# Banded attention: the division by the sums moved from VectorE to GpSimd, and the output copies moved ahead of the transposed tiles' copies

## What is computed

```python
s = einsum('bnqkgd,bnjkd->bnkgqj', qb, kb) * (Dh ** -0.5)
s = s - slopes * dist;  s = where(in_window & real_key, s, -inf)
m = maximum(s.max(axis=-1), sink)
p = exp(s - m[..., None])
denom = p.sum(axis=-1) + exp(sink - m)
p = p / denom[..., None]
o = einsum('bnkgqj,bnjkd->bnqkgd', p, vb)
```

## Time and profile before

| what | value |
|---|---|
| time, median of 3 runs | 3200.48 us (3200.15 to 3201.1) |
| time of the profiled execution | 3194.09 us |
| its span (first to last instruction) | 3192.2 us |
| TensorE busy | 3029.1 us |
| VectorE busy | 1512.5 us |
| ScalarE busy | 738.1 us |
| GpSimd busy | 15.9 us in 30 instructions |

### The profile page before, as it was taken

One profiled execution on the slowest core, in us unless ns is written; L12 is line 12 of the kernel. 1 busy time (PEld: TensorE's weight loads), 2 busy tenths in 40 slices (PEclk: granted clock), 3 DMA queues, 4 the chain that ended last, 5 costly groups with the idle time before them and its releaser, 6 DMA issues.

```text
span 3192.2 us, 37105 instructions
## 1 busy us (share of the span) xinstructions
PE 3029.1 (95%) x15055; PEld 2235.0 (70%) x15055; DVE 1512.5 (47%) x2327; ACT 738.1 (23%) x1397; POOL 15.9 (0%) x30
## 2 busy tenths in 40 slices
PE   6999999999899999979999998999999997899999
PEld 4888888868755888854443433468888845788887
DVE  2577766726566345451101122356554427645544
ACT  4343434321076110120000012332000025300001
POOL 0000000000000000000000000000000000000000
PEclk8999999999999999989999999999999998999999
DMA  5145334342200122249999981102222220122221
GB/s 224 71 182 196 139 139 177 120 161 74 96 14 8 78 108 80 79 163 391 421 422 422 422 342 69 53 27 79 80 79 106 80 81 27 53 79 80 81 104 53
DMA packets 64234, 451.80 MB, mean 142 GB/s; under 512 B 7248, under 2 KB 7264, under 8 KB 11216
## 3 DMA queue, kind: packets, MB, share of 16 engines
q1 hardware_dynamic: 61200, 439.38, 34.5%
q0 software_dynamic: 2080, 7.11, 0.7%
q10 hardware_dynamic: 800, 3.15, 0.3%
HBM read 445.41 MB, written 2.10 MB: 140 GB/s over the span
## 4 chain that ended last, share of the span: by engine, by line
PE 85%; DMA 6%; DVE 5%; ACT 2%; issue 1%; DVEq 1%; SPq 0%; PEldq 0%; PEld 0%; POOL 0%; ACTq 0%; POOLq 0%
PE PS L228 77%; DMA ring<-stream 4%; PE PS L1508 1%; PE PS L1618 1%; PE PS L1601 1%; DVE arena L1570 1%; DMA hT<-stream 1%; DVE stat L1627 1%; PE PS L2273 1%; PE PS L2293 1%; DVE stat L2620 0%; PE PS L2276 0%; DVE PS L2618 0%; ACT arena L1537 0%; PE PS L873 0%
## 5 line engine op out<-in xcount | busy, mean ns | idle before, releaser
L228 PE MATMUL PS<-arena 128*128 128x256 f32 (+3 forms) x4960 | 986.2, 389 | 9.0 <-issue 4.9
L228 PEld LDWEIGHTS PS<-arena 128*128 128x128 f32 (+1 forms) x4960 | 744.3, 183 | 237.8 <-issue 156.6
L228 PE MATMUL PS<-arena,ring 128*128 128x256 f32 (+1 forms) x1992 | 466.7, 390 | 0.3 <-issue 0.3
L228 PE MATMUL PS<-hT,ring 128*128 128x256 f32 (+1 forms) x1504 | 409.8, 428 | 23.7 <-ACT hT L323 11.5
L228 PEld LDWEIGHTS PS<-arena,ring 128*128 128x128 f32 x1992 | 377.6, 190 | 74.6 <-issue 26.5
L228 PEld LDWEIGHTS PS<-hT,ring 128*128 128x128 f32 x1504 | 289.8, 194 | 130.2 <-issue 86.7
L228 PE MATMUL PS<-xT,arena 128*128 128x256 f32 x1056 | 232.0, 379 | 0.0
L228 PEld LDWEIGHTS PS<-xT,arena 128*128 128x128 f32 x1056 | 200.6, 190 | 28.1 <-issue 1.0
L228 PE MATMUL PS<-ring,arena 128*32 128x512 f32 (+3 forms) x1088 | 198.2, 590 | 12.1 <-issue 6.5
L228 PE MATMUL PS<-hT,arena 128*128 128x256 f32 (+1 forms) x864 | 195.2, 442 | 1.3 <-DMA hT<-stream 1.3
L2092 DVE TENSOR_TENSOR arena<-arena,PS 128x512 f32<-128x512 f32 x16 | 11.0, 688 | 368.3 <-PE PS L228 368.3
(11 more groups left out here) (307 smaller groups left out, 2946.9 us busy)
## 6 DMA issues: line engine op xcount, KB each, us to landing
ring<-stream SPq DMA_DIRECT2D x283, 1024.0 KB, 6.9
arena<-stream SPq DMA_DIRECT2D x96, 1024.0 KB, 18.8
hT<-stream SPq DMA_DIRECT2D x32, 1024.0 KB, 18.7
arena<-stream SPq DMA_DIRECT2D x8, 512.0 KB, 5.0
arena<-x ACTq DMA_DIRECT2D x1, 2048.0 KB, 10.6
xT<-stream SPq DMA_DIRECT2D x2, 1024.0 KB, 15.4
arena<-arena POOLq DMA_DIRECT2D x16, 128.0 KB, 2.6
arena<-x POOLq DMA_DIRECT2D x1, 2048.0 KB, 12.5
```

The costliest lines, as they stand in the source:

```text
L228: ins = nc.tensor.matmul(out_, lhsT, rhs, start=start, stop=stop_, **kw)
```

## The change

In the attention with a sink, DVE stops after the reciprocal (which now overwrites the sums) and signals the new semaphore `a_r`; GpSimd waits for it, does the four multiplications in place, and signals `a_n`, for which the transposes wait as before. ScalarE's output copies of a finished head group are issued ahead of the copies of the current unit's transposes. The sink's value gets four places in turn (in the rows `RECIP` and `SINK`) in place of two. The two semaphores of `iota` and `router` become one, `in_route`, and both waits are for both loads.

```diff
+        def sink_of(u):
+            return stat[:, RECIP + u % 4 // 2, u % 2, :]
...
+            a_r = sem(f"{name}_r") if sink else None
...
-                        nc.scalar.activation(col(SINK, u), col(SINK, u), ACT.Exp)
+                        nc.scalar.activation(sink_of(u), sink_of(u), ACT.Exp)
...
                     if u + 1 < n:
                         exps(u + 1)
+                    for i, m in enumerate(last_unit):
+                        if m == u - 2 and sink:
+                            outputs(i)
                     copies(u)
                     for i, m in enumerate(last_unit):
-                        if m == u - 2:
+                        if m == u - 2 and not sink:
                             outputs(i)
...
                 def normalise(u):
                     v.wait_ge(a_e, u + 1)
                     if sink:
-                        nc.vector.tensor_tensor(col(SUM, u), col(SUM, u), col(SINK, u), ALU.add)
+                        nc.vector.tensor_tensor(col(SUM, u), col(SUM, u), sink_of(u), ALU.add)
                         v.drain()
+                    if sink:
+                        nc.vector.reciprocal(col(SUM, u), col(SUM, u)).then_inc(a_r, 1)
+                        return
...
+            def pool_(pool):
+                for u in range(n):
+                    pool.wait_ge(a_r, u + 1)
+                    for h in range(nh):
+                        x = norm_io(u, h)
+                        ins = nc.gpsimd.tensor_scalar(x, x, col(SUM, u)[:, h:h + 1], None, ALU.mult)
+                    ins.then_inc(a_n, 1)
...
-            pe.wait_ge(in_router, 16)
+            pe.wait_ge(in_route, 32)
...
-            v.wait_ge(in_iota, 16)
+            v.wait_ge(in_route, 32)
...
             pool.dma_start(snk[:, 0, :], sinks).then_inc(in_swa, 16)
+            swa_att_pool(pool)
```

More of the change, by code:

```diff
@@ L199, in build @@
         evac_done = sem("evac_done")
-        in_const, in_vec, in_x, in_c, in_cst2, in_acst, in_iota = (sem(n) for n in
-            ("in_const", "in_vec", "in_x", "in_c", "in_cst2", "in_acst", "in_iota"))
+        in_const, in_vec, in_x, in_c, in_cst2, in_acst, in_route = (sem(n) for n in
+            ("in_const", "in_vec", "in_x", "in_c", "in_cst2", "in_acst", "in_route"))
         vec_t, vec_ok, cs_ok, ada_sel = (sem(n) for n in ("vec_t", "vec_ok", "cs_ok", "ada_sel"))
@@ L1558, in peak @@
                     v.wait_ge(a_s, u + 1)
-                    maximum(v, u, S2[u % 2], col(MAX, u), col(NEGMAX, u), col(SINK, u)).then_inc(a_m, 1)
+                    maximum(v, u, S2[u % 2], col(MAX, u), col(NEGMAX, u), sink_of(u)).then_inc(a_m, 1)
                 def normalise(u):
@@ L1578, in dve_ @@
                         peak(u + 2)
-            return pe_, act_, dve_, a_o, a_s
+            def pool_(pool):
[5 more added lines that the diff above has]
+                    ins.then_inc(a_n, 1)
+            return pe_, act_, dve_, a_o, pool_ if sink else a_s
         def tile_of(a, i):
@@ L1852, in build @@
         idxu = sb("idxu", [NE, CAP], u32)
-        in_router, r_lg, r_sum, r_mx, r_ex, r_aff, r_affT, r_tt, r_blk, r_row, r_ok = (sem(n) for n in
-            ("in_router", "r_lg", "r_sum", "r_mx", "r_ex", "r_aff", "r_affT", "r_tt", "r_blk", "r_row", "r_ok"))
+        r_lg, r_sum, r_mx, r_ex, r_aff, r_affT, r_tt, r_blk, r_row, r_ok = (sem(n) for n in
+            ("r_lg", "r_sum", "r_mx", "r_ex", "r_aff", "r_affT", "r_tt", "r_blk", "r_row", "r_ok"))
         e_g, e_xs, e_gu, e_sg, e_hid, e_T, e_hT, e_dn, e_ys, e_cb, e_acc = (sem(n) for n in
@@ L2624, in swa_maximum @@
             return nc.vector.tensor_tensor(extra, neg, snk[:, 0, 4 * g:4 * g + 4], ALU.add)
-        swa_att_pe, swa_att_act, swa_att_dve, swa_out, _ = attention(
+        swa_att_pe, swa_att_act, swa_att_dve, swa_out, swa_att_pool = attention(
             "swa", 16, 4, swa_score, swa_chunk, swa_dest, [[u] for u in range(16)], swa_value,
@@ L2707, in _ @@
             pool.wait_ge(x_ok, 1)
-            pool.dma_start(iota_s, iota).then_inc(in_iota, 16)
-            pool.dma_start(rw, router).then_inc(in_router, 16)
+            pool.dma_start(iota_s, iota).then_inc(in_route, 16)
+            pool.dma_start(rw, router).then_inc(in_route, 16)
             pool.wait_ge(x_ok, 2)
```

## The result

The changed kernel is slower: 3216.1 us in the median of 6 executions (3211.94 to 3217.66) against 3200.32 (3191.82 to 3201.69) for the kernel before, a ratio of 1.0052 [1.0039, 1.0065]. Forecast were 3197.2 us and a range up to 3211; the time lies beyond it. The profiled execution of the changed kernel took 3211.94 us, its span is 3209.7.

What follows compares the result with a forecast made beforehand. VectorE was taken to pace each 17.74 us head group; a ring of 16.87 us saves 0.87 a group, 3.3 us over 15 / 4 groups, all else 0: 3200.5 - 3.3 = 3197.2 us. Range 3190 to 3211.

Steps and rivals of the forecast that it cites:

- 4P + 4P': GpSimd's eight scalings in a head group: P a full one, taken as 0.46 us, P' a short one, 0.37.
- rival 2: Each GpSimd scaling costs like a DMA issue, 0.80 us: 3209.6 us, chance 0.25; its lower-clock extreme 3230 us, 0.03.
- rival 1: GpSimd scales as quickly as VectorE (P = 0.30, P' = 0.22): 3192.6 us, chance 0.3.
- the even ring: Loop of waits through peaks of even units: 11.51 + 2H + 8P, 16.09 us a head group.
- the tail: After the last unit's exponentials, scalings free the transposes after 2.7 us; they started 3.3 us after before: nothing added.
- the ring: Loop of waits from VectorE's reciprocal through GpSimd's scalings and TensorE to VectorE's peak, two turns a head group, at full clock.
- H: Pair of hand-offs, VectorE to GpSimd and GpSimd to TensorE: taken as 0.45 us, bounds 0.10 and 0.60.
- the odd ring: Loop of waits through peaks of odd units, the slower: 12.65 + 2H + 4P + 4P', 16.87 us a head group.
- VectorE's own 16.5: VectorE's own work for a head group in the kernel before: 16.5 us of 17.74.
- The output copies: ScalarE's output copies, issued earlier: the values' wait for them disappears, with TensorE's 1.87 us and the slow clock behind it.
- rival 4: VectorE's small SBUF instructions at a peak's end and GpSimd's scalings exclude each other, meeting over P = 0.56; no own chance.
- rival 3: GpSimd's first scaling stalls once for a code fetch, 7.2 us: 3204.4 us, chance 0.05.

Runs made afterwards that it cites:

- e5: The changed kernel with 12 idle transposes of the identity (the fill) on TensorE ahead of each unit's wait for the scalings: 3204.26 us, ratio 1.0017 to the kernel before.
- e4: The changed kernel with VectorE waiting for the last scaling before its sums for the next stage: 3209.48 us, ratio 1.004 to the kernel before.
- e9: The changed kernel with GpSimd scaling only 128 columns of each head, plus 8 idle transposes ahead of each unit's wait: 3204.44 us, ratio 1.0012 to the kernel before.
- e14: The changed kernel with 8 idle transposes a unit, a first signal after two scalings, and VectorE's last sums behind the last scaling: 3201.32 us, ratio 1.0003.
- e10: The kernel before with output copies moved first and 6 idle transposes ahead of each unit's wait, no scalings on GpSimd: 3190.82 us, ratio 0.9978.
- e1: The kernel before with only the output copies moved ahead of the unit's copies, nothing on GpSimd: 3194.61 us, ratio 0.9989.
- e2: The changed kernel with the output copies back behind the unit's copies: 3218.52 us, ratio 1.0066 to the kernel before.
- e11: As e10, but VectorE multiplies three of four heads and GpSimd one: 3193.53 us, ratio 0.9982 to the kernel before.
- e3: The changed kernel with GpSimd scaling only the first 128 of a full unit's 256 columns: 3205.65 us, ratio 1.0028 to the kernel before.
- e13: The kernel before, output copies at their old place, with 6 idle transposes ahead of each unit's wait: 3191.91 us, ratio 0.9986.

## Why the prediction was wrong

**The step that failed** is "Between them stands ScalarE's pass over the same tiles [...]. I take it, 0.46 and 0.37". The term 4P + 4P' is 5.98 us a group, not 3.32. P + P' = 1.495 is just over the point 1.48 that rival 2 named as its decision. The reason given against that rival, that a DMA issue is no pass over data, was true and no evidence: it said nothing on the price of a pass. Nor was 0.80 the price of every issue: the same engine's issue for the router weights took 0.54 us in that trace. And not all its rows were slow, as said against rival 1: four memsets of 128x1 took 0.10 each. GpSimd's time has a part that grows with the columns: (0.907 - 0.588) / 128 = 2.49 ns for each, and 0.27 us besides, so it is also no flat 0.80 as rival 2 had it. This step alone would not have left the range: with 0.907 in the forecast's own sum the even ring becomes the slower, 11.51 + 0.90 + 8 x 0.907 = 19.67 us, 7.2 us more in all, and the tail 1.2 more: 3209 us.

The page "GPSIMD Engine Reference" of the Trainium skill, section 3.1, would have had P at 0.22 to 0.38 us, by the forecast's estimate; 0.907 is over twice its upper end. Here the measurement decides. (From 0.22 to 0.38, with half of it for a short scaling, the ring would be 1.0 to 2.0 us below the forecast's, not 0.6 to 1.9.)

**"That is why the ring is counted at full clock"** failed too, and took the time from there out of the range. Longer waits of TensorE for GpSimd brought the lower level with them, 1.7 us a group (20.59 against e5's 18.93), and 8.8 us of the stage in all. The forecast had the mechanism only as the extreme of rival 2, at 0.03 and 20 us. It was the larger half: of 16.3 us the fill gives 8.8 back and e4's wait 2.7; what is left is put down to the ring's own length, with the end. These shares overlap, since each of them changes how long TensorE waits.

**H** was 0.14 to 0.15 us for a pair, near the lower bound 0.10, not 0.45. That made the forecast's ring 0.6 us too long, and hid a little of P's error.

**The ring's form and fixed pieces** were right for the odd ring, in the last group: 18.93 measured for 18.91 (e5), 17.66 for 17.61 (e9), 18.31 for 18.1 (e14). The even ring was put too long. It counts a short unit's scores at the full 1.17 us and its values at 0.51, and e5's rows have 0.76 (2705.93 to 2706.69) and 0.59. With the measured scalings and hand-offs its sum is 19.05 us, above the 18.93 measured; put right it is 18.7, under the odd one. VectorE's own 16.5 was right, and e10 reached it.

**The output copies.** Right that their wait goes (the changed kernel's list of waits, and e1). Wrong that the time goes with it: e1 gains 1.4 us of stage and still has transposes at the lower clock, until something keeps TensorE busy (e10).

**The tail** was put at nothing. Behind the last unit's sum the transposes start 6.27 us later, 3.31 before; VectorE's row and TensorE's:

```profile
2739.13 0.16 DVE L1572 TENSOR_TENSOR stat<-stat 128x4 f32<-128x4 f32 x1 [5.09 <-ACT arena L1531]
```

```profile
2745.40 1.97 PE L1513 MATMUL PS<-C,arena 128*128 128x128 f32 x8 [3.35 <-POOL arena L1596]
```

Of the 3.0 us more, 2.1 are the scalings slowed by VectorE's early sums (5.71 for 3.63). The forecast had seen that VectorE reaches these sums earlier and priced it only as no gain.

**The shared port** (rival 4) was looked for at the wrong place. While GpSimd scales (7.23 us for eight, from 2689.70), VectorE's small instruction follows its reduction as closely as before:

```profile
2689.70 7.23 POOL L1596 TENSOR_SCALAR arena<-arena,stat 128x256 f32<-128x256 f32 x8 [4.43 <-DVE stat L1575]
```

```profile
2690.80 1.22 DVE L2639 TENSOR_REDUCE stat<-PS 128x4 f32<-128x1024 f32 x1
2692.10 0.16 DVE L2641 SCALAR_TENSOR_TENSOR stat<-stat,arena 128x4 f32<-128x4 f32 x1
```

1.30 us from the one to the other, the same as in the kernel before. In other traces two such instructions were longer beside scalings, 0.41 us for 0.16 (e2, 2716.53) and 0.33 (e5, 2669.81). The large instructions met: the sums (5.71 us for 3.63) and, in e11, VectorE's multiplications. "SBUF — State Buffer", section "Who interferes with whom", of the Trainium skill has an instruction of VectorE with two SBUF inputs contend with a GpSimd one that reads SBUF, calls the shared ports an exclusive lock, and says of VectorE's two-port modes that whoever issues first has them for the whole instruction while the other "fully blocks". The rows agree that these pairs interfere. One scaling that lost 1.58 us beside sums of 1.21 fits a full block. The others do not: both engines lose only a part (1.45 us for 1.23 in the first sum; 1.21 us for three multiplications and 1.06 for one scaling, started together in e11).

**The first use** (rival 3) cost nothing: 2.36 us for the first four, 2.35 for later ones. **The merged semaphore** cost nothing that shows, as put: TensorE's wait is put down to the router weights, the later of the two loads, and is 6.38 us where it was 6.26 in the trace before.

```profile
1392.28 1.08 PE L1896 MATMUL PS<-hT,arena 128*32 128x512 f32 x4 [6.38 <-DMA arena<-router]
```

## What to carry to other kernels

Before work leaves a busy engine, ask whether it leaves the ring: here it stayed on every unit's path, and only its price changed, from 0.285 to 0.907 us. An engine for which the trace has no such instruction is not to be priced by another engine's row; by this ring the move could only have matched VectorE's 16.5 us with P + P' at (16.5 - 12.93) / 4 = 0.89, and a single probe of one scaling would have told it. Where TensorE waits between small pieces, count its pieces at both clock levels, because a shorter wait elsewhere may be paid back by the clock (e1, e3), and a few idle transposes in the gap can be worth more than the edit itself (e10 against e1: 4.0 us of stage). They are not free where they outlast the wait: 0.9 us in one group of e5.

## What the hardware showed unexpectedly

- A GpSimd multiplication of f32 by one number a row took 0.907 us for 256 columns and 0.588 for 128, which is 0.27 us and 2.49 ns for each column by these two widths, and three times VectorE's 0.285 at 256 columns; its hand-offs are short, 0.09 us from VectorE and 0.06 us to TensorE.
- The same ring with more work on TensorE is faster: 20.59 us a group at a granted clock of 0.81 in the window, 18.93 at 1.00. Of the kernel before, with the fill alone (e13) or the output copies first alone (e1) the clock of the stage is 0.87 or 0.84; with both (e10) 0.95.
- VectorE and GpSimd slow each other when both work on SBUF with large operands, by 0.1 us (VectorE, 456 ns in the mean for 350 in the kernel before) and 0.15 us (GpSimd) an instruction in e11 and by up to 2.1 us for four in the changed kernel. Instructions with 128x4 operands mostly kept their 0.16 us, with single ones at 0.33 and 0.41. What decides the size stayed open.
- Executions of one kernel differ by 5 us and more on either side of their median (3185.03 to 3196.15 in e10), so that the stage in one trace and the median don't always say the same (e13).
